# A transformer kernel's last stage: first expert search over one head, half of the first queries computed inside the gather, keys fetched earlier, ring slots freed by the splits

## The reference

```python
def peer_layer(h, w_q, sub_keys, u_tab, v_tab):
    ...
    q = (hf @ w_q).reshape(T, PEER_HEADS, 2, PEER_DQ // 2)
    s = jnp.einsum('thpd,hpnd->thpn', q, sub_keys)
    sc, idx = lax.top_k(s, PEER_TOPK)
    cand = (sc[:, :, 0, :, None] + sc[:, :, 1, None, :]).reshape(T, PEER_HEADS, PEER_TOPK * PEER_TOPK)
    cidx = (idx[:, :, 0, :, None] * PEER_NKEYS + idx[:, :, 1, None, :]).reshape(T, PEER_HEADS, PEER_TOPK * PEER_TOPK)
    top_sc, pos = lax.top_k(cand, PEER_TOPK)
    eidx = jnp.take_along_axis(cidx, pos, axis=-1)
    gate = jax.nn.softmax(top_sc.astype(jnp.float32), axis=-1).astype(h.dtype)
    ...
        act = jax.nn.gelu(jnp.einsum('thkd,td->thk', u_tab[eb], hb), approximate=False)
        return jnp.einsum('thk,thkd->td', gb * act, v_tab[eb])
```

## Time and profile before

| | before |
|---|---|
| median of 3 runs | 3825.77 us |
| profiled execution, its span | 3827.33 us, 3825.6 us |
| PE, DVE, ACT, POOL busy | 88%, 59%, 17%, 49% |
| gather rows (q0) | 73728 packets, 536.90 MB |
| all other loads and stores (q1) | 196496 packets, 204.53 MB |
| w_out loads, issue to landing (median) | 6.4 us |
| DMA rate in slices 28 to 38 of 40 | 402 to 422 GB/s |

### The profile page before, as it was taken

The page is one execution under the profiler, slowest core; times in us unless marked ns, Lnnn a source line. Parts: engine busy times, 40 slices in busy tenths (PEclk is TensorE's granted clock), DMA queues, the critical chain, the costliest instruction groups (busy, mean ns, idle before and its releaser), DMA issues. The chain is left out here.

```text
span 3825.6 us, 34103 instructions
## 1 busy us (share of the span) xinstructions
PE 3351.4 (88%) x12241; PEld 2130.1 (56%) x12241; DVE 2252.0 (59%) x4233; ACT 661.0 (17%) x1353; POOL 1885.9 (49%) x1174
## 2 busy tenths in 40 slices
PE   7997999999988999999999889699987777777776
PEld 5434966887665478877877667544443333333323
DVE  3834534334643243357935677487778777778754
ACT  2122222111215221111112331111010010000101
POOL 2211307989410179887877448144444444444441
PEclk9997999999989999999999999899999999999999
DMA  4430002232330122322432211699999999999995
GB/s 146 152 123 1 1 23 86 90 99 98 117 105 1 33 82 94 99 88 77 130 113 86 77 34 58 213 387 400 415 405 421 421 422 421 421 419 402 422 421 237
DMA packets 274581, 749.91 MB, mean 196 GB/s; under 512 B 13049, under 2 KB 200962, under 8 KB 208898
## 3 DMA queue, kind: packets, MB, share of 16 engines
q0 software_dynamic: 73728, 536.90, 34.0%
q1 hardware_dynamic: 196496, 204.53, 16.9%
q10 hardware_dynamic: 4210, 6.56, 0.5%
HBM read 739.56 MB, written 8.39 MB: 196 GB/s over the span
## 5 line engine op out<-in xcount | busy, mean ns | idle before, releaser
L840 POOL TENSOR_TENSOR split_arena<-weight_ring,ones 128x1024 fp32r<-128x1024 f32 x218 | 541.8, 2485 | 589.0 <-PE bank L948 322.6
L899 POOL DMA_INDIRECT arena<-in_peer_uv,rstd x388 | 432.3, 1114 | 632.9 <-PE bank L1435 558.9
L1027 PE MATMUL bank<-split_arena 128*128 128x512 f32 x1744 | 685.4, 393 | 0.0
L2530 DVE CUSTOM_DVE_ANT_0 arena<-arena,branch 128x1024 f32<-128x1024 f32 x388 | 475.0, 1226 | 241.2 <-DMA arena<-in_peer_uv,rstd 238.0
L842 POOL TENSOR_TENSOR split_arena<-weight_ring,split_arena 128x1024 fp32r<-128x1024 f32 x218 | 553.2, 2538 | 17.1
L1435 PE MATMUL bank<-arena,row_diagonals 128*128 128x512 f32 x776 | 390.4, 650 | 128.7 <-DVE row_diagonals L2514 128.5
L1025 PE MATMUL bank<-split_arena 128*128 128x512 f32 x1072 | 421.5, 393 | 21.5 <-DVE split_arena L1970 14.0
L1026 PE MATMUL bank<-split_arena 128*128 128x512 f32 x1072 | 418.9, 391 | 0.0
L1435 PE MATMUL bank<-arena,level_mask 128*128 128x512 f32 x776 | 354.7, 600 | 47.9 <-DVE level_mask L2514 47.9
L1027 PEld LDWEIGHTS bank<-split_arena 128*128 128x128 f32 x1744 | 329.5, 189 | 72.0
L1435 PEld LDWEIGHTS bank<-arena,row_diagonals 128*128 128x128 f32 x776 | 153.5, 206 | 357.3 <-DVE row_diagonals L2514 190.0
(11 more groups left out here) (376 smaller groups left out, 4884.7 us busy)
## 6 DMA issues: line engine op xcount, KB each, us to landing
weight_ring<-in_w_up SPq DMA_DIRECT2D x32, 1024.0 KB, 5.4
weight_ring<-in_w_down SPq DMA_DIRECT2D x32, 1024.0 KB, 5.0
weight_ring<-in_w_in SPq DMA_DIRECT2D x32, 1024.0 KB, 5.7
weight_ring<-in_ada_w SPq DMA_DIRECT2D x24, 1024.0 KB, 7.7
weight_ring<-in_peer_wq SPq DMA_DIRECT2D x16, 1024.0 KB
weight_ring<-in_w_in_a SPq DMA_DIRECT2D x13, 1024.0 KB, 5.2
weight_ring<-in_w_out SPq DMA_DIRECT2D x12, 1024.0 KB, 6.4
weight_ring<-in_w_in_b SPq DMA_DIRECT2D x10, 1024.0 KB, 5.1
```

The costliest lines, as they stand in the source:

```text
L840: pool.tensor_tensor(hi, part, bc_mid(ones[:], DT), ALU.mult).then_inc(split_hi, 1)
L899: pool.indirect_dma_start(row_slots[slot_of[r]], None, a["peer_uv"], bass.IndirectOffsetOnAxis(ap=experts[n % 2][:, c:c + 1], axis=0)).the ...
L1027: return pe.matmul(psum[t.bank][:], hi, a_lo[:, k, :], start=False, stop=k == DT - 1)
L2530: dve.tensor_tensor_reduce(row, row, h_tok[:, r // NE, :], 1.0, 0.0, ALU.mult, ALU.add, dots[:, i % 4, j:j + 1]).then_inc(dot_ready, 1)
```

## The change

`first_units` are computed one unit (one head) at a time into a bank's half. Only units 0 to 3 come before the loop over groups; the eight halves of units 4 to 7 are put at groups 1, 3, ... 15 (`first_at`). Block 0 is searched in five parts instead of four (`parts`): head 0, head 1, heads 2 and 3, 4 and 5, 6 and 7. The first two run before the loop, and POOL waits for head 0 alone before row 0 and for head 1 before row 16. The second pass moves to groups 17 to 79, token transposes, scores and searches of later blocks by 7 to 15 groups, and `EARLY` from row 136 to 168. The keys go to the memory-key and memory-value tiles in two DMAs, issued once the last recurrent head is gated, ahead of the w_out_2 loads. `load` waits for the split of the slot's former unit, where that one is split, and no longer for its matmuls. The MLP's own loop of loads is as before.

```diff
-EARLY = 136
+EARLY = 168
...
+        FIRST = PH // 2
...
+        parts = [[(0, 1), (1, 1)] + [(h, 2) for h in range(2, PH, 2)]] + [[(h, 2) for h in range(0, PH, 2)]] * (TT - 1)
+        searched = {}
+        for n in range(TT):
+            for g in range(len(parts[n])):
+                searched[n, g] = len(searched) + 1
...
-        for g in range(PH // SG):
-            first_tiles.append(half_tile(first_units[SG * g + SG - 1], 1, g))
-            if g == 0:
-                tok_turns[0] = [aux(2 + i) for i in range(2)]
-            peer_scores[0].append(aux(4 + g % 2))
+        for j, b in enumerate((0, 1, 6, 7)):
+            first_tiles.append(half_tile(first_units[j], 1, b))
+        tok_turns[0].append(aux(2))
+        peer_scores[0].append(aux(4))
+        tok_turns[0].append(aux(3))
+        peer_scores[0] += [aux(5), aux(4)]
+        for j in range(FIRST, PH):
+            first_tiles.append(half_tile(first_units[j], 1, 2 + j % 2))
...
-        query_at = {2 + 2 * y: y for y in range(2 * HP)}
-        turn_at = {7 + 4 * (2 * (n - 1) + i): (n, i) for n in range(1, TT) for i in range(2)}
-        score_at = {(BLK_GRP * (n - 1) + 16 * g + (20 if n == 1 else 28)): (n, g) for n in range(1, TT)
-                    for g in range(PH // SG)}
+        first_at = {1 + 2 * y: y for y in range(2 * (PH - FIRST))}
+        query_at = {17 + 2 * y: y for y in range(2 * HP)}
+        turn_at = {20 + 4 * (2 * (n - 1) + i): (n, i) for n in range(1, TT) for i in range(2)}
+        score_at = {BLK_GRP * (n - 1) + 16 * g + 35: (n, g) for n in range(1, TT) for g in range(len(parts[n]))}
+        score_at.update({11: (0, 3), 19: (0, 4)})
...
-        key_rows = arena[:, F2:F2 + HP * P].rearrange("p (i d) -> p i d", d=P)
+        key_rows = [m[:, :, :, :].rearrange("p a t n -> p (a t n)").rearrange("p (i d) -> p i d", d=P) for m in (memk, memv)]
...
-        search_at = {(0, 1): (0, 1), (0, 2): (10, 1), (0, 3): (20, 1)}
+        search_at = {(0, 2): (0, 1), (0, 3): (15, 1), (0, 4): (24, 1)}
         for n in range(1, TT):
-            for g in range(PH // SG):
-                search_at[n, g] = (BLK_GRP * (n - 1) + 16 * g + 32, 2)
+            for g in range(len(parts[n])):
+                search_at[n, g] = (BLK_GRP * (n - 1) + 16 * g + 39, 2)
...
+                if u.before and u.before.split is not None:
+                    sp.wait_ge(split_ready, u.before.split + 2)
+                elif u.before:
                     sp.wait_ge(half_done, 2 * (u.before.u + 1))
...
+            sp.wait_ge(mix_ready, LH + HH)
+            for i, rows in enumerate(key_rows):
+                sp.dma_start(rows, a["peer_keys_2"].rearrange("o h s n d -> n (o h s) d")[:, PH * i:PH * (i + 1), :]).then_inc(
+                    s_keys, 16)
             for u in wo_units:
                 load(u)
-            for t in wo_tiles:
-                have(sp, t)
-            sp.dma_start(key_rows, a["peer_keys_2"].rearrange("o h s n d -> n (o h s) d")).then_inc(s_keys, 16)
...
-                if c % (SG * TOPK) == 0:
-                    pool.wait_ge(id_ready, n * (PH // SG) + c // (SG * TOPK) + 1)
+                for g, (h, _) in enumerate(parts[n]):
+                    if c == h * TOPK:
+                        pool.wait_ge(id_ready, searched[n, g])
...
+            def first_half(j, h):
+
+                u, t = first_units[j], first_tiles[j]
+                if h == 0:
+                    pe.wait_ge(landed[u.slot], 16 * u.load)
+                    free(pe, t)
+                for k in range(DT):
+                    if j == 0 and h == 0:
+                        normed(k)
+                    m = pe.matmul(blk(psum[t.bank], h), block_of(u, k, h * P), H[:, k, 0:P], start=k == 0, stop=k == DT - 1)
+                m.then_inc(half_done, 1)
+
+            def token_turn(n, x):
+                turn(tok_turns[n][x], [blk(H[:, 4 * x + j, :], n) for j in range(4)])
+
+            for j in range(FIRST):
+                for h in range(2):
+                    first_half(j, h)
+                if j == 0:
+                    token_turn(0, 0)
+                    key_scores(0, 0)
+                    token_turn(0, 1)
+                elif j > 1:
+                    key_scores(0, j - 1)
             pre[0] += 1
             for i in range(NGRP):
                 sum_rows(i)
+                if i in first_at:
+                    first_half(FIRST + first_at[i] // 2, first_at[i] % 2)
                 if i in query_at:
                     query_piece(query_at[i])
                 if i in turn_at:
-                    n, x = turn_at[i]
-                    turn(tok_turns[n][x], [blk(H[:, 4 * x + j, :], n) for j in range(4)])
+                    token_turn(*turn_at[i])
...
+            def take_first(j):
+                t = first_tiles[j]
                 full(act, t)
-                act.activation(pq_f[:, 4 * g:4 * (g + 1), 0:P], chunks(psum[t.bank]), ACT.Copy).then_inc(bank_out[t.bank], 1)
-                if g == 0:
-                    for i in range(2):
-                        take(tok_turns[0][i], h_tok[:, 0, 512 * i:512 * (i + 1)])
-                take(peer_scores[0][g], score_s[:, 512 * g:512 * (g + 1)])
+                act.activation(pq_f[:, 2 * j:2 * j + 2, 0:P], chunks(psum[t.bank])[:, 0:2, :], ACT.Copy).then_inc(
+                    bank_out[t.bank], 1)
+
+            def take_scores(n, g):
+                head, heads = parts[n][g]
+                t = peer_scores[n][g]
+                full(act, t)
+                act.activation(score_s[:, 2 * P * head:2 * P * (head + heads)], psum[t.bank][:, 0:2 * P * heads],
+                               ACT.Copy).then_inc(bank_out[t.bank], 1)
+
+            for j in range(FIRST):
+                take_first(j)
+                if j == 0:
+                    take(tok_turns[0][0], h_tok[:, 0, 0:512])
+                    take_scores(0, 0)
+                    take(tok_turns[0][1], h_tok[:, 0, 512:1024])
+                elif j > 1:
+                    take_scores(0, j - 1)
             gate_exp(0, 0)
+            gate_exp(0, 1)
             for i in range(NGRP):
                 act.wait_ge(dot_ready, GROUP * (i + 1))
                 act.activation(row_act[:, i % 4, :], dots[:, i % 4, :], ACT.Gelu).then_inc(gelu_ready, 1)
+                if i - LAG in first_at and first_at[i - LAG] % 2:
+                    take_first(FIRST + first_at[i - LAG] // 2)
...
-            for _ in search(0, 0):
-                pass
-            normalize_gates(0, 0)
+            for g in range(2):
+                for _ in search(0, g):
+                    pass
+            for g in range(2):
+                normalize_gates(0, g)
```

More of the change, by code:

```diff
@@ L1451, in query_piece @@
                     m.then_inc(half_done, 1)
-            for g, t in enumerate(first_tiles):
-                for x in range(2 * SG):
-                    u, h = first_units[SG * g + x // 2], x % 2
-                    if h == 0:
-                        pe.wait_ge(landed[u.slot], 16 * u.load)
-                    if x == 0:
-                        free(pe, t)
-                    for k in range(DT):
-                        if g == 0 and x == 0:
-                            normed(k)
-                        m = pe.matmul(blk(psum[t.bank], x), block_of(u, k, h * P), H[:, k, 0:P], start=k == 0, stop=k == DT - 1)
-                    m.then_inc(half_done, 1)
-                if g == 0:
-                    for i in range(2):
-                        turn(tok_turns[0][i], [blk(H[:, 4 * i + j, :], 0) for j in range(4)])
-                key_scores(0, g)
+            def first_half(j, h):
[19 more added lines that the diff above has]
+                    key_scores(0, j - 1)
             pre[0] += 1
@@ L1856, in _ @@
                     n, g = score_at[i - LAG]
-                    act.wait_ge(id_ready, (n - 1) * (PH // SG) + g + 1)
-                    take(peer_scores[n][g], score_s[:, 512 * g:512 * (g + 1)])
+                    head, heads = parts[n][g]
+                    if n:
+                        act.wait_ge(id_ready, max(searched[n - 1, x] for x, (h, _) in enumerate(parts[n - 1]) if h < head + heads))
+                    take_scores(n, g)
                 if i in take_at:
@@ L2452, in search @@
             def search(n, g):
-                halves = slice(2 * SG * g, 2 * SG * (g + 1))
-                heads = slice(SG * g, SG * (g + 1))
-                es = slice(SG * g * TOPK, SG * (g + 1) * TOPK)
-                ne = SG * TOPK
+                head, nh = parts[n][g]
+                halves = slice(2 * head, 2 * (head + nh))
+                heads = slice(head, head + nh)
+                es = slice(head * TOPK, (head + nh) * TOPK)
+                ne = nh * TOPK
+                sums = work_b[:, 0:nh * TOPK * TOPK]
                 have(dve, peer_scores[n][g])
-                yield from best16(2 * SG, top_v[:, halves, :], top_i[:, halves, :], s3[:, halves, :], left_keys)
```

(3 more changed lines are left out.)

41 lines of the change are left out of this document (20 added, 21 removed).

## The result

The changed kernel takes 3802.95 us, the median of 4 runs (3795.72 to 3804.03), against 3825.84 of 4 runs before. The ratio is 0.9936, 95% interval 0.9919 to 0.9953: faster by 0.6%. 3805 was forecast, with a range of 3792 to 3817. The profiled execution took 3795.72 us, its span is 3794.0, the lowest of the four.

The account below looks back on a forecast made before the run. The last third was taken as bound by the gather's DMA stream, with a late start and a hole; 20.5 us off the profiled 3827.3 gives 3806.8, which, as that execution lay 1.5 above the median, became 3805, range 3792 to 3817.

Parts of the forecast that it names:

- The first row: At the gather's start: searching head 0 alone, with keys on chip, issues row 0 12.4 us earlier.
- the key fetch: Ahead of the first query unit: keys on chip early, of which some 2.4 us matter for row 0.
- Row 8: First gather row needing a used slot: issued at 2448.1 instead of 2483.10, 35.0 us earlier.
- the two ends named for a lone gather row: Row 8's issue: 2448.1 if DVE's readiness decides, 2449.7 if a lone row takes 12.5 us to land.
- What had to be given back: In the gather loop: ten loads instead of six, 160 rows on eight slots, leaving 20.5 us gained at row 504.
- the middle: At row 504: 20.5 us earlier, taken between the readings of 22.4 and 18.7.
- the first end: Rows 8 to 168: rows and loads alike cost 2.594 us each, putting row 504 22.4 us earlier.
- The ring: Upstream weight loads: freeing slots by splits brings loads earlier, given 0 us, bounds 0 and 1.1.
- Rival 1: Between rows 7 and 8: the idle DMA hole stays, only the start counts; gain 10.3, 3815.5 us; chance 0.16.
- Rival 2: Rows on eight slots: loads hide under a slot-set pace of 2.716 us a row; 28.8 earlier, 3797; chance 0.10.
- Rival 3: Groups 9, 13, 17: PE waits for late weights; slower from 38 us landing, 3838 us at 42; chance 0.04.
- Rival 4: At the start or upstream: an unseen wait or slower upstream loads cancel the gain; 3822 to 3830 us; chance 0.07.

Follow-up runs that it names:

- g1: The kernel before, unchanged, profiled a second time; 3826.65 us in one run.
- g3: The changed kernel with the two key DMAs issued after the w_out_2 loads and the last projection's tiles; 3798.49 us, ratio 0.9932.
- e3: The changed kernel with row 0 held until head 1 is searched too; 3802.34 us, ratio 0.9937.
- f2: The changed kernel without the second pass's eight query weight loads, PE multiplying what the slots hold; 3779.22 us, ratio 0.9872.
- f3: The changed kernel with twelve slots from row 296 on instead of 168; 3798.89 us, ratio 0.9919.
- e1: The kernel before with only the ring edit, slots reloaded once their former unit is split; 3825.47 us, ratio 0.9995.
- e4: The changed kernel with the queries of units 4 to 7 and their ACT copies put ahead of the loop again; 3819.85 us, ratio 0.9984.
- g4: The changed kernel with units 4 to 7 each loaded once for both passes, four loads fewer; 3785.47 us, ratio 0.99.
- e2: The changed kernel with ring slots freed by the matmuls again, as in the old kernel; 3801.46 us, ratio 0.9931.
- g2: The changed kernel, unchanged, run a third time; 3798.1 us, ratio 0.9933.
- f1: The changed kernel, unchanged, run again; 3799.16 us, ratio 0.9919.
- f4: The changed kernel with the last columns of blocks 1 to 3 normed in the loop, at groups 9 to 12; 3798.1 us, ratio 0.9916.

## Why the prediction was right, and where it was not

**The first row.** Predicted 12.4 us earlier; measured from the norm's factor 33.5 - 21.1 = 12.4 (by g1, before's second profile, 35.3 - 21.1 = 14.2). One head's search was put at 9.8 and takes 9.9. That the key fetch decides some 2.4 us of it was right in size (g3: 2.0 at row 0, 2.4 at the end) and not in makeup: the forecast had PE start late at full clock, g3 has it start less late and run the unit slower.

**Row 8.** Predicted 35.0 earlier, measured 75.3 - 41.1 = 34.2. Of the two ends named for a lone gather row, DVE's readiness decided, as taken. The bound beside it, 12.5 us for such a row, was far off: e3 shows 5.9 from issue to dot. The Trainium skill (DMA: Bandwidth & Descriptors, Anatomy of one DMA) gave an estimate of 4.4, 1.5 under the measured 5.9 and nearer than the bound from the rows.

**What had to be given back: the term that was mis-sized.** The step took the middle between two ways to read 347.6 us for 128 rows, and the second of them was wrong. It made twelve-slot rows and eight-slot rows equal and left 4.1 us to a load. f2 shows 2.3 to 2.5 a load and f3 0.03 to 0.04 a row for the slots, so the first end (2.594 for rows and loads alike, 22.4 at row 504) was close and the middle 2 too low. Measured at row 504 is 1341.9 - 1316.5 = 25.4. The stretches show where the other 3 lie: rows 8 to 168 are 441.0 by the first end and take 439.2, 442.3 and 439.1 in three profiles; rows 168 to 504 were forecast at 838.2 and take 836.2, 834.6 and 836.0. One reason is in the rate of rows 8 to 136: before, which starts them behind the hole, moves 397 GB/s there, after 409, and the forecast carried before's pace over. In the first profile the stretches give 1.8 + 2.0, less the 0.8 that row 8 fell short.

**The profile of before.** It was at the short end of its own scatter: 1417.8 from norm to end, where e1 and g1, the same there, have 1421.1 and 1422.3. By means of three the change is worth 1420.4 - 1391.8 = 28.6 in this stretch. The medians of whole executions give 22.9, 30.2 and 27.0 in three series. So 3805 came near the first 3802.95 with some luck: the gain is nearer 27 than 21, and the other series' 3799.16 and 3798.1 lie at the low side of the range.

**Where the 28.6 come from.** 21.7 by the units moved into the loop, with their copies on ACT (e4). The remaining 7 are the start: 2.4 by the keys (g3) and the rest, some 4.5, by the search over head 0 alone, which fits what e3 has lost at row 136 (4.5); its 6.7 at the end hold some 2 us of scatter. All of these are differences of single profiles; the three of after end 1.8 apart, before's and e1's 4.5.

**The ring.** Given 0 with bounds 0 and 1.1; e1 measures -0.05% with an interval across no change (-5.0 to +1.5 us), wider than these bounds, so it doesn't test them.

**The rivals.** Rival 1, the hole stays: refuted by the share of 1.02 to 1.04 over the old gap. It was also priced too kindly, at a gain of 10.3 by the start alone: e4, which has row 0 early and the hole in place, gains 5.3 in the medians and 6.9 in the stretch. Rival 2, the loads hide: refuted by f2, though its price, 3797, is nearer to 3799.16 and 3798.1 than the forecast is. Rival 3, weights too late: refuted, with 1.5 us of waits, none in the loop, and 26.3 us as the longest landing under the 31 that a unit has. Rival 4 had nothing for it. The query weights' packets, put at 1.1 KB, are 1.04 KB by the earlier trace rows; nothing hangs on it.

**Open.** Rows 136 to 168 take 82 to 86 us in every kernel with the second pass moved. At 2.52 a row they would take 80.6. The traces show part of the reason. In the last four of these rows PE waits 3.0 to 3.8 us for DVE's diagonals in every kernel but g4. The eight matmul instructions behind that wait take 3.70 us in after, e2, g2, g3 and e4; they take 5.40 in f1, f2, f3 and f4 and 6.42 in e3. The granted clock of the whole stretch is 1.00 in the first five and 0.96 to 0.98 in the others. PE's timeline of after:

```profile
2874.76 3.70 PE L1450 MATMUL bank<-arena,level_mask 128*128 128x512 f32 x8 [3.08 <-DVE level_mask L2563]
```

and of f1, the same kernel:

```profile
2879.66 5.40 PE L1450 MATMUL bank<-arena,level_mask 128*128 128x512 f32 x8 [3.05 <-DVE level_mask L2563]
```

So after, e2, g2 and g3 pass the stretch in 82.2 to 82.4 us and f1, f3, f4 and e3 in 84.8 to 85.6 (f2 83.9, e4 84.4, g4 81.9), which is where most of f1's three us at row 168 come from. Why the clock falls behind the same wait in one execution and not in another stays open. So does what paces the rows ahead of it: in after, rows 136 to 164 have PE busy 68.3 of 69.6 us and the DMA share at 1.01, both full.

## What to carry to other kernels

Where the end of a kernel is one long stream of transfers, count its bytes first and its holes second: a MiB less was worth 2.3 to 2.6 us in the stretch (f2, g4), while a first transfer 12.4 us earlier whose buffers were not reused sooner by as much was worth 6.9 (e4). Move work that isn't needed for the first transfer behind it, into a loop whose engines have room, and check that weights fetched under the stream are issued one landing time ahead of use. And before two profiles are subtracted, find an instruction ahead of the change that both have, and see from a second profile of the same kernel how far it moves by itself.

## What the runs showed of the hardware

A gather DMA of 1 MiB on idle DMA engines is usable 5.9 us after its issue; under the full stream it takes 20.3. A weight load of 1 MiB in packets of about 1 KB lands 25.2 us after its issue under the gather, but leaving it out shortens the stream by no more than a gather row in packets of 7.3 KB takes: 2.3 to 2.5 us (f2) against 2.52. Eight buffers of 1 MiB cost 0.03 to 0.04 us a row against twelve (f3). The time ahead of the last norm differs by up to 5.8 us between executions (2402.0 to 2407.8), while row 0 follows the norm's factor by 21.1 us in all eight profiles of kernels that start as after does. And 2.75 us of PE waiting for a DMA were followed by a mean granted clock of 0.65 over its first query unit, which took 5.63 us instead of 3.81 (g3). Such a drop isn't certain: behind a wait of 3.05 us PE ran eight matmul instructions in 5.40 us (f1), behind one of 3.08 us in 3.70 (after), in the same kernel.
